# Squares of a finished tile moved ahead of the next slab's split, and the last tile's squares added by VectorE

## The reference

```python
def rms_norm(x, g):
    y = xf * lax.rsqrt(jnp.mean(xf * xf, axis=-1, keepdims=True) + EPS)
    return y.astype(x.dtype) * g

def ada_norm(x, g, shift, scale):
    return rms_norm(x, g) * (1.0 + scale) + shift

# first_block, each layer l; hctx alike
    x = x + 0.5 * mx[:, 2] * swiglu(ada_norm(x, norm_g[l, 0], mx[:, 0], mx[:, 1]), ffn_w_in[l, 0], ffn_w_out[l, 0])
    hx = ada_norm(x, norm_g[l, 1], mx[:, 3], mx[:, 4])
    ...
    x = x + mx[:, 5] * yx
    x = x + 0.5 * mx[:, 8] * swiglu(ada_norm(x, norm_g[l, 2], mx[:, 6], mx[:, 7]), ffn_w_in[l, 1], ffn_w_out[l, 1])
return rms_norm(x, final_g)

def _layer_norm(x, g, b):
    mu = jnp.mean(xf, -1, keepdims=True)
    var = jnp.mean(jnp.square(xf - mu), -1, keepdims=True)
    return ((xf - mu) * lax.rsqrt(var + LN_EPS) * g + b).astype(x.dtype)

# second_block, each layer i; ctx alike in layer 0
    x = _layer_norm(alpha * x + g1 * y, ln1_g[i], ln1_b[i])
    x = _layer_norm(alpha * x + g2 * _mlp(x * (1 + sc2) + sh2, mlp_w1[i], mlp_w2[i]), ln2_g[i], ln2_b[i])
```

## Time and profile before

| | |
|---|---|
| Median of 3 runs | 3057.37 us (3055.07 to 3059.44) |
| The profiled execution | 3059.67 us, span 3057.9 |
| Granted clock of TensorE, mean | 0.956 |
| PE busy | 2855.6 us, 93% of the span |
| DVE, ACT, POOL busy | 1948.3, 1152.7, 338.1 us |
| Share of PE in the chain that ended last | 82% (DVE 6%, ACT 6%, POOL 2%) |

### The profile page before, as it was taken

One profiled execution on the slowest core, in us unless ns is written; L12 is line 12 of the kernel. 1 busy time (PEld: TensorE's weight loads), 2 busy tenths in 40 slices (PEclk: granted clock), 3 DMA queues, 4 the chain that ended last, 5 costly groups with the idle time before them and its releaser, 6 DMA issues.

```text
span 3057.9 us, 38748 instructions
## 1 busy us (share of the span) xinstructions
PE 2855.6 (93%) x15476; PEld 2378.6 (78%) x15476; DVE 1948.3 (64%) x3265; ACT 1152.7 (38%) x1901; POOL 338.1 (11%) x396
## 2 busy tenths in 40 slices
PE   5999999988899999999999989989989999898797
PEld 4888887545888888888887889976678888876797
DVE  6788845645687866878654765544466775457554
ACT  3322234443422224222244555434362223535552
POOL 0000010321100001000011110100130001200201
PEclk8999999988999999999999999999989999899898
DMA  5666522101355634555331245521134442243453
GB/s 213 216 217 225 197 79 90 49 28 42 124 205 196 211 118 152 205 197 210 118 122 62 70 143 182 166 73 38 56 111 161 170 154 94 85 106 84 129 187 108
DMA packets 125427, 412.18 MB, mean 135 GB/s; under 512 B 25232, under 2 KB 27280, under 8 KB 124608
## 3 DMA queue, kind: packets, MB, share of 16 engines
q1 hardware_dynamic: 109696, 353.08, 34.1%
q0 software_dynamic: 15552, 56.63, 5.3%
HBM read 408.61 MB, written 1.05 MB: 134 GB/s over the span
## 4 chain that ended last, share of the span: by engine, by line
PE 82%; DVE 6%; ACT 6%; POOL 2%; issue 2%; DMA 2%; SPq 0%; POOLq 0%; ACTq 0%; DVEq 0%
PE bank L2291 25%; PE bank L2293 25%; PE bank L2292 25%; PE bank L2528 2%; POOL sb_temp L1242 2%; ACT sb_split_high L1361 1%; DVE sb_split_low L1771 1%; DMA sb_ada_ffn<-ada 1%; PE bank L2676 1%; DVE sb_h_low L1858 1%; DMA sb_na_raw<-na_rpb 1%; PE bank L2489 1%; DVE sb_temp L1852 1%; ACT sb_x_res L1439 1%; PE bank L2611 0%
## 5 line engine op out<-in xcount | busy, mean ns | idle before, releaser
L2291 PE MATMUL bank<-sb_h_high,sb_split_high 128*128 128x256 f32 (+1 forms) x3040 | 1062.9, 350 | 75.4 <-DVE sb_h_low L1866 35.2
L2292 PE MATMUL bank<-sb_h_low,sb_split_high 128*128 128x256 f32 (+1 forms) x3040 | 1041.1, 342 | 0.0
L2293 PE MATMUL bank<-sb_h_high,sb_split_low 128*128 128x256 f32 (+1 forms) x3040 | 1040.1, 342 | 0.0
L1771 DVE TENSOR_TENSOR sb_split_low<-sb_raw,sb_split_high 128x1024 fp32r<-128x1024 f32 x515 | 635.9, 1242 | 233.7 <-ACT sb_split_high L1361 230.8
L2291 PEld LDWEIGHTS bank<-sb_h_high,sb_split_high 128*128 128x128 f32 x3040 | 592.1, 195 | 162.3 <-issue 41.5
L1361 ACT ACTIVATE sb_split_high<-sb_raw 128x1024 fp32r<-128x1024 f32 x515 | 537.0, 1051 | 336.6 <-DMA sb_raw<-weights 336.5
L2292 PEld LDWEIGHTS bank<-sb_h_low,sb_split_high 128*128 128x128 f32 x3040 | 594.0, 195 | 63.9 <-issue 0.5
L2293 PEld LDWEIGHTS bank<-sb_h_high,sb_split_low 128*128 128x128 f32 x3040 | 592.7, 195 | 65.0
L1785 DVE CUSTOM_DVE_ANT_0 sb_temp<-sb_ada_ffn,sb_cond_ffn 128x1024 bf16<-128x1024 f32 x398 | 468.1, 1220 | 23.3 <-DMA sb_ada_ffn<-ada 14.7
L1915 DVE SCALAR_TENSOR_TENSOR sb_x_res<-bank,sb_gates,sb_x_res 128x256 f32<-128x256 f32 x320 | 145.2, 480 | 241.2 <-PE bank L2293 240.8
L2291 PE MATMUL bank<-sb_hidden_high_ffn,sb_split_high 128*128 128x512 f32 (+1 forms) x830 | 279.9, 337 | 0.0
(11 more groups left out here) (270 smaller groups left out, 2950.7 us busy)
## 6 DMA issues: line engine op xcount, KB each, us to landing
sb_raw<-weights SPq DMA_DIRECT2D x515, 512.0 KB, 3.3
sb_ada_ffn<-ada SPq DMA_DIRECT2D x114, 512.0 KB, 4.3
sb_ada_ffn<-ada POOLq DMA_DIRECT2D x90, 512.0 KB, 3.6
sb_ada_mlp<-ada POOLq DMA_DIRECT2D x18, 512.0 KB, 3.5
sb_ada_mlp<-ada SPq DMA_DIRECT2D x18, 512.0 KB, 4.2
sb_cond_ffn<-cond SPq DMA_DIRECT2D x3, 1024.0 KB, 5.4
sb_na_raw<-na_rpb SPq DMA_DIRECT2D x32, 96.0 KB, 6.0
sb_x_res<-tokens SPq DMA_DIRECT2D x1, 2048.0 KB, 15.3
```

Source lines behind the costliest of these rows:

```text
L1771: do.tensor_tensor(m.low[i][:, :], m.raw[i][:, :], m.high[i][:, :].bitcast(F32), ALU.subtract).then_inc(*dve.mark("split_low", s))
L2291: do.matmul(out, ah, bh, start=start and j == 0, stop=False)
L2292: do.matmul(out, ah, bl, start=False, stop=False)
L2293: last = do.matmul(out, al, bh, start=False, stop=stop and j == len(terms) - 1)
```

## The change

In `down_piece` and `out_piece` the steps `square` (or `add_mean`) now stand ahead of `done`. The last add of the squares, k = 7, leaves POOL and goes to DVE, with a signal of its own, `last_added`, for which PE's `sum_of_squares` waits. DVE waits for POOL's add of k = 6 and for ACT's square of k = 7. In layer norms the same add is called at the end of `centre`.

```diff
--- before.py
+++ after.py
@@ -473,8 +473,8 @@
 def down_piece(f, c, k, p, ring, square):
     bank, n = ring.next(), SIZES[f][c]
     done = [down_slab(f, c, b) for b in range(k * n, k * n + n) if b % 8 == 7]
-    steps = [("down", f, c, k, p, bank), ("add", f, (f, c, k), k, p, bank), *part_done(p, *done)]
-    return steps + [(square, NORM_AFTER[f], k, s) for s in STREAMS_OF[p]] if square else steps
+    squares = [(square, NORM_AFTER[f], k, s) for s in STREAMS_OF[p]] if square else []
+    return [("down", f, c, k, p, bank), ("add", f, (f, c, k), k, p, bank), *squares, *part_done(p, *done)]
 
 
 def square_step(stage):
@@ -526,7 +526,7 @@
     done = part_done(p, slab) if not halves or k % 2 else []
     final = half == 1 or not halves
     squares = [(square_step(name), NORM_AFTER[name], k, s) for s in STREAMS_OF[p]] if final else []
-    return [("out", name, k, half, p, bank), ("add", name, (name, k, half), k, p, bank), *done, *squares]
+    return [("out", name, k, half, p, bank), ("add", name, (name, k, half), k, p, bank), *squares, *done]
 
 
 def out_pieces(name, ring, tail):
@@ -946,7 +946,7 @@
     "gla_gate", "ctx2", "na_bv", "rpb0", "rpb1", "stored",
     "gemm", "summed", "swapped", "gates_turned", "scored", "turned", "weighed", "squares_added", "g_spread",
     "spread", "decay_in", "keys_turned", "inner_scored", "state_in", "inner_out", "chunk_in", "chunk_out",
-    "split_high", "split_low", "cond_silu", "ada_dot", "ada_block", "mods", "scales", "gates", "squared", "added", "mean", "root", "rstd", "rstd_spread",
+    "split_high", "split_low", "cond_silu", "ada_dot", "ada_block", "mods", "scales", "gates", "squared", "added", "last_added", "mean", "root", "rstd", "rstd_spread",
     "scaled", "h_high", "h_low", "silu", "relu", "relu_squared", "hidden_raw", "hidden_high", "hidden_low", "x_new",
     "x_final", "x_scaled", "plain", "centred", "ln_scaled", "ln_out", "fm_act", "fm_dve", "tm_act", "tm_dve",
     "gate_act", "gate_dve", "fcol", "floor_act", "lambda_dve", "lambda_act", "rope_sin", "rope_cos", "roped",
@@ -1242,6 +1242,8 @@
         do.tensor_tensor(acc, other if k == 1 else acc, new, ALU.add).then_inc(*pool.mark("added", (kind, tag, k, p)))
 
     def square(tag, k, p):
+        if k == DT - 1:
+            return
         pool.wait_ge("squared", (tag, k, p))
         add_up("square", tag, k, p, m.squares[k % 2][:, COLS[p]], m.squares[0][:, COLS[p]])
 
@@ -1860,6 +1862,15 @@
             *dve.mark("h_low", (tag, k, p), (tag, k)))
         last_low[0] = tag, k, p
 
+    def square(tag, k, p):
+
+        if k < DT - 1:
+            return
+        acc = m.acc[:, COLS[p]]
+        dve.wait_ge("added", ("square", tag, k - 1, p))
+        dve.wait_ge("squared", (tag, k, p))
+        do.tensor_tensor(acc, acc, m.squares[k % 2][:, COLS[p]], ALU.add).then_inc(*dve.mark("last_added", (tag, p)))
+
     def low_of(tag, k, p, src):
 
         dve.wait_ge("h_high", (tag, k, p))
@@ -1876,6 +1887,7 @@
             x = m.x[:, k, COLS[p]]
             do.scalar_tensor_tensor(x, m.bank[6 + p][:, 0:NC_TOK], -1.0 / D, x, ALU.mult, ALU.add).then_inc(
                 *dve.mark("centred", (tag, k, p)))
+        square(tag, DT - 1, p)
 
     def layer_norm(tag, p):
         _, layer, which = LAYER_NORMS[tag]
@@ -2246,7 +2258,7 @@
                 *dve.mark("x_final", k))
 
     work = {"split": split, "ada": ada, "mods": mods, "scales": scales, "gates": gates, "mean": mean, "rstd": reciprocal, "scaled": scaled,
-            "put_low": put_low, "plain_put": plain_put, "centre": centre, "layer_norm": layer_norm, "mult": mult, "relu": relu,
+            "put_low": put_low, "plain_put": plain_put, "square": square, "centre": centre, "layer_norm": layer_norm, "mult": mult, "relu": relu,
             "hidden_low": hidden_low, "add": add, "fm_copy": fm, "tm_copy": tm, "forget": forget, "lambda": lam,
             "rope": rope, "conv": conv, "da_scores": da_scores, "da_normalise": da_normalise, "da_combine": da_combine,
             "ml_weights": ml_weights, "ml_normalise": ml_normalise, "ml_combine": ml_combine, "even_stat": even_stat,
@@ -2331,7 +2343,7 @@
         read[6] = "mean", (tag, BOTH)
 
     def sum_of_squares(tag, p):
-        pe.wait_ge("added", ("square", tag, DT - 1, p))
+        pe.wait_ge("last_added", (tag, p))
         free(6 + p)
         for j in range(NC_TOK // P):
             last = do.matmul(m.bank[6 + p][:, NC_TOK + j:NC_TOK + j + 1], m.acc[:, COLS[p]][:, j * P:(j + 1) * P], m.C("ones")[:, 0:1],
```

## The result

| | before | after |
|---|---|---|
| Median, 8 runs each | 3057.21 us (3054.32 to 3061.75) | 3065.73 us (3061.99 to 3068.28) |
| Ratio | | 1.0023 (95% interval 1.0014 to 1.0033) |
| The profiled execution: time, span | 3059.67, 3057.9 | 3061.99, 3060.2 |
| Granted clock, mean | 0.956 | 0.956 |
| PE, DVE, ACT, POOL busy | 2855.6, 1948.3, 1152.7, 338.1 | 2851.7, 1949.1, 1151.7, 308.3 |

The change makes the kernel slower by 0.23%, between 4 and 10 us by the interval; the forecast was 3064.8.

What follows compares the result with a forecast made beforehand. TensorE's (PE's) idle time was taken to bound the kernel, 46.1 us of it waiting for POOL's sums in 12 places. 6.9 + 0.7 + 1.1 + 1.0 - 2.4, unrounded +7.4, on 3057.37 gave 3064.8 us; range 3057 to 3070.

Steps and rivals of the forecast that it cites:

- The loop's size: Latent end of ffn00: ACT and DVE wait on each other, `split_low` 1.91 after each x add; tile 7's x add +3.26.
- The last link: From tile 7's x add to PE's sum: 1.44 instead of 2.38; net +2.3 at each of three places, +6.9.
- Why POOL's add was slow: POOL's last add took 1.33 because it ran beside DVE's `split_low`; layer-norm adds with DVE idle took 0.84.
- n02: Norm after the even mixer: x add +2.6, last link -1.5, context sum -0.4, together +0.7.
- n12: Norm after the odd mixer: three loop turns of 3.45 each put DVE's mean +1.1 later.
- The final norm: After ffn11: ACT squares first, then splits three times, so the mean comes later, +1.0.
- Layer norms: Six sums, only the last add moves to DVE: -0.4 each, -2.4; DVE's standing still there is free.
- Rival 1: Clock stays up at two layer-norm stalls, shortened from 2.16 to about 1.76: +3.6, 3061.0; chance 0.17.
- rival 2: Clock also falls at the final norm, where PE's wait grows from 1.85 to 2.8: +9.4, about 3067; chance 0.12.
- third sign of being wrong: The prediction is wrong if the clock after the two layer-norm stalls has changed.
- Rival 4: PE's gemm, not the loop, sets tile 7's x add; only last links count: -6.3, 3051.1; chance 0.08.
- Rival 3: Delay made up between tiles 3 and 4: each place costs 0.9, not 2.3; sum +3.2, 3060.6; chance 0.15.

Runs made afterwards that it cites:

- order_only: The kernel before with only the new order (squares ahead of done); POOL still adds the last squares. 3070.26 us against 3056.73, ratio 1.0043.
- last_tile: The changed kernel, but with the new order for tile 7 alone; last add on DVE. 3047.18 us against 3056.73, ratio 0.9968.
- final_only: The kernel before with the new order at the final norm alone; every add of squares on POOL. 3057.80 us against 3056.61, ratio 1.0004.
- ln_only: The kernel before with only the six layer-norm sums' last add on DVE; old order. 3056.57 us against 3057.26, ratio 0.9995.
- before_again: The kernel before, unaltered, run again for a second trace. Ratio 0.9997.
- after_again: The changed kernel, unaltered, run again for a second trace. 3064.13 us against the kernel before's 3056.73, ratio 1.0028.
- add_only: The kernel before with only the last add moved to DVE; old order. 3055.80 us against 3056.73, ratio 0.9995.
- n01_only: The kernel before with the whole change at the norm after ffn00 alone. 3059.35 us against 3057.26, ratio 1.0006.
- n10_only: The kernel before with the whole change at the norm behind ffn01 alone. 3056.74 us against 3056.61, ratio 1.0002.
- out_only: The kernel before with the whole change only at the norms after the even and odd mixers. 3059.14 us against 3056.61, ratio 1.0007.
- best: The kernel before with, except at the final norm, tile 7's squares ahead of done and the last add on DVE. 3046.87 us against 3057.26, ratio 0.9963.
- rms_tail: The kernel of best, but with the layer norms' last add left on POOL. 3045.85 us against the kernel before's 3056.61, ratio 0.9969.

## Why the prediction was right, point by point

The sum of steps was +7.4; measured +7.0 by the ratio (4.3 to 10.1) and +8.5 by the medians, and +8.6 by the ratio in the second set. By its own steps:

- **The loop's size** (1.91 from x add to `split_low`): 1.91 or 1.92 four times. Tile 7's x add +3.26 predicted, +3.18 measured. Shown by order_only (loop alone, no faster than the change) and last_tile (loop opened, faster than before).
- **The last link** (2.38 to 1.44): in after, 442.06 - 440.55 = 1.51, DVE's add 0.43 as taken from the earlier trace rows. Net per place +2.3 predicted, +2.31, +2.31 and +2.32 measured. A detail of the text was wrong: the wait before the sum was to be 5.6. It is 3.4. Of the rest, 1.82 is a stall for `h_low` further ahead (2.19 instead of 0.37), and 0.43 is PE's own work: it is busy for 17.82 instead of 17.39 in this stretch, at a mean granted clock of 0.90 instead of 1.00. I had followed the x adds through the loop and not the `h_low` that DVE does between them.
- **Why POOL's add was slow**: order_only has the same add at 0.73 once no `split_low` is beside it, in step with the reason given from the earlier trace rows. A reading was off: the 0.84 for one of the first six adds of a layer norm is a sixth of a folded row; the add itself takes 0.72, and 0.14 lie between two of them.
- **n02**: latent stretch +2.6 - 1.5 = +1.1 predicted, +1.16 measured; the context sum's wait of 0.41 became 0.14, -0.3 for the -0.4 predicted. Not predicted: the head piece behind the sum takes 5.75 instead of 6.14.
- **n12**: +1.1 predicted, +1.4 measured. The mis-sized term is a turn of the loop, 3.45 predicted for all three. The first is 3.45, and in the two behind it `split_low` loses 0.17 and 0.16 to a POOL add that began before it. Missed altogether: the lower clock behind n12's longer waits. With it the +1.4 at the mean is +2.3 to +2.4 at the final sum; how much of these 0.9 is the clock's, beyond the 0.5 in the spread, is not taken apart.
- **The final norm**: +1.0 predicted; the mean behind tile 7's x add 5.33 in final_only and in after, 4.36 before, +0.97. final_only shows it alone, with 2.2 more behind it for the clock in its trace.
- **Layer norms**: -0.4 at four of the six by the waits, in after and in ln_only. By PE's waits at all six sums after is 4.0 under the first trace of before and 2.4 under the second; -2.4 was predicted from the first. That DVE's standing still there is free fits: in after it waits 4.18, where it idled for 4.37 before.
- **Rival 1 and rival 2, the clock**: a step that failed is the one behind the rivals' chances. I read from one trace that a wait of 2.16 loses the clock and one of 1.85 keeps it. before_again has the 1.85 again, with the clock lost. What stood in the earlier trace rows was one course of several that the same kernel takes. And the stall of 2.16 at ln00's latent sum did not become 1.76: it is gone, and the clock behind it is up. In after, the sum and the four us behind it, with the columns of the earlier trace rows:

```profile
2249.28 0.50 PE L2349 MATMUL bank<-sb_const,sb_temp 128*128 128x1 f32 x4
...
2249.00:2253.00 4.00, 4.00 (x37) 1.00 0.01 2
```

  That is the prediction's own third sign of being wrong, and rival 1's course at this stall. At the other, ln01's context sum, the wait is 1.75 and the clock in 2603 to 2607 0.70, with 0.50 in 2598 to 2602 before. From ln00's context sum to ln01's latent sum after takes 412.5, against 415.6 and 413.2 in the two traces of before. So most of rival 1's price is a difference between two courses of the kernel before. Rival 2's 2 us are seen in final_only's trace and in neither of after: from n12's sum to ln00's context sum final_only has 436.6, the five traces of kernels that are unchanged there have 432.8 to 433.4, and the two of after 435.3 and 435.1. In after, +1.0 is the final norm's, and some +1.1 n12's (the mean 0.56 further behind the sum, and 0.5 in the spread).
- **Rival 4** (tile 7 paced by PE's gemm): fell; after's x add at 440.55 waits for nothing of PE. **Rival 3** (delay made up between tiles 3 and 4): fell; from tile 3's x add to tile 4's it is 4.97 in after and 3.57 before, so all of the 1.40 stays.
- **The range**: its lower end, 3057, was to lie half-way between rivals 3 and 4. That is 3055.9.

The sum of the local steps as measured is 6.9 + 1.2 - 0.3 + 1.4 + 1.0 - 2.4 = +7.8, with the layer norms taken against before_again. With what follows behind n02 (-0.4) and n12 (+0.9) it is +8.3. That the forecast lies so near the time has some luck in it: the clock moves the stretches between the norms by more than most single steps. In its two traces the changed kernel is 4.9 and 5.2 behind by n12's sum, and only 2.3 and 4.5 at the end.

| kernel | sum of steps, as expected | measured, us (interval) |
|---|---|---|
| after | +7.4 | +7.0 (+4.3 to +10.1) |
| after_again | +7 to +8.5 | +8.6 (+5.2 to +11.6) |
| before_again | 0 | -0.9 (-3.7 to +1.8) |
| order_only | +11 | +13.1 (+8.9 to +17.4) |
| add_only | -3.0 | -1.5 (-4.0 to +1.2) |
| last_tile | -6.3 | -9.8 (-13.8 to -6.1) |
| ln_only | -2.4 | -1.5 (-4.0 to +1.2) |
| n01_only | +2.3 | +1.8 (-0.9 to +4.6) |
| n10_only | +2.3 | +0.6 (-1.8 to +3.4) |
| out_only | +2.2 | +2.1 (-0.6 to +4.6) |
| final_only | +1.0 | +1.2 (-1.5 to +4.0) |
| best | -9.2 | -11.3 (-15.0 to -7.3) |
| rms_tail | -5.3 | -9.5 (-12.5 to -6.1) |

The measured column is the ratio less one, times 3057. Single places cost too little to be seen one by one in the time, though each local step shows in the trace to 0.02; the sums of several are seen.

## What to carry to other kernels

When two engines each run their work in strict order, moving a step ahead of another can close a loop between them: look what the moved step waits for, what on the other engine waits for the step that it was moved ahead of, and what stands behind that. A move that pays at the last tile can cost at each tile ahead of it, so make it at the last one alone: here the same two edits, with the new order for tile 7 alone, turned +0.23% into -0.3%. And take a second trace of the unchanged kernel before pricing anything by the clock of a single stretch.
